# Where the context's tiles begin modulo 512 bytes in a two-block transformer kernel

## The reference

```python
# block 1 (depth 1)
h = rmsnorm(x) * (1 + sc1) + sh1
proj = h @ w_in                      # attention, gated delta rule
x = x + g1 * (concat(y_attn, y_delta) @ w_out)
x = x + g2 * ((silu(h2 @ w_gate) * (h2 @ w_up)) @ w_down)
x = rmsnorm(x)
# block 2, for i in range(2); m from c, mc from c_ctx
h  = ffn_half_step(h,  ..., w13_ffn1[i], w2_ffn1[i])   # sequence, 512 tokens
hc = ffn_half_step(hc, ..., w13_ffn1[i], w2_ffn1[i])   # context, 256 tokens
z  = modulate(rms_norm(h),  ...) @ w_in[i]
zc = modulate(rms_norm(hc), ...) @ w_in[i]             # last layer: key and value columns only
k, v from z and zc; y = concat(fourier(z), attend(q, k, v), sgu(z), pooling(z)) @ w_out[i]
h  = h + m[5] * y
h  = ffn_half_step(h, ..., w13_ffn2[i], w2_ffn2[i])
# the same mixer and second half step for the context, in layer 0 only
```

## The kernel before, in words

| tile | before | after the edit |
|---|---|---|
| weight slots `high`, `low`, `stage`, `tmp`, `eye`, `ones` | 128 | 128 |
| sequence: `hn`, `hidden`, `mixed` | 384 | 384 |
| context: `hn`, `hidden`, `mixed` (from `phase_base`, and in the mixer) | 64 | 384 |
| `keys`, `values`, `token_dft`, first `weights_t` of the context | 64 | 384 |
| `queries`, `scores` and `weights_t` of the sequence, `q_rank`, `fourier`, `rope` | 448 | 256 |
| first block: `attention_out`, `silu_z`, `delta_qkv` | 64 | 384 |

## Time and profile before

### The profile page before, as it was taken

One profiled execution on the slowest core, in us unless ns is written; L12 is line 12 of the kernel. 1 busy time (PEld: TensorE's weight loads), 2 busy tenths in 40 slices (PEclk: granted clock), 3 DMA queues, 4 the chain that ended last, 5 costly groups with the idle time before them and its releaser, 6 DMA issues. The chain is left out here.

```text
span 3632.5 us, 49233 instructions
## 1 busy us (share of the span) xinstructions
PE 3440.5 (95%) x19911; PEld 2834.4 (78%) x19911; DVE 2148.4 (59%) x4936; ACT 1031.5 (28%) x1604; POOL 131.9 (4%) x116
## 2 busy tenths in 40 slices
PE   5889889999999999899999999989999999999998
PEld 4655867887888888774688888878888886578887
DVE  6454656567667575764455767676766636544334
ACT  3354023222421212242432121222122125432222
POOL 0012010000000000100000000010000010000000
PEclk9998879999999999898999999989999999999999
DMA  8532024444234343330023434333333313023331
GB/s 176 146 95 67 3 58 131 121 132 112 86 99 116 99 114 95 99 87 17 24 64 99 111 93 115 97 107 87 106 105 103 106 53 110 13 73 95 94 104 64
DMA packets 646938, 333.94 MB, mean 92 GB/s; under 512 B 31659, under 2 KB 642935, under 8 KB 646456
## 3 DMA queue, kind: packets, MB, share of 16 engines
q1 hardware_dynamic: 645812, 330.63, 33.3%
q10 hardware_dynamic: 900, 0.18, 0.0%
HBM read 328.61 MB, written 2.77 MB: 91 GB/s over the span
## 5 line engine op out<-in xcount | busy, mean ns | idle before, releaser
L2105 PE MATMUL psum<-hn_high,high 128*128 128x512 f32 (+1 forms) x3136 | 1117.7, 356 | 9.4 <-DVE low L2550 9.3
L2107 PE MATMUL psum<-hn_high,low 128*128 128x512 f32 (+1 forms) x3136 | 1107.2, 353 | 0.0
L2106 PE MATMUL psum<-hn_low,high 128*128 128x512 f32 (+1 forms) x3136 | 1107.0, 353 | 0.0
L2635 DVE SCALAR_TENSOR_TENSOR partial<-stage,cond,partial 128x128 f32<-128x128 f32 x2592 | 701.8, 346 | 0.0
L2105 PEld LDWEIGHTS psum<-hn_high,high 128*128 128x128 f32 x3136 | 592.0, 189 | 116.1 <-issue 20.8
L2107 PEld LDWEIGHTS psum<-hn_high,low 128*128 128x128 f32 x3136 | 595.6, 190 | 82.0
L2106 PEld LDWEIGHTS psum<-hn_low,high 128*128 128x128 f32 x3136 | 591.7, 189 | 79.6 <-issue 0.5
L2550 DVE TENSOR_TENSOR low<-stage,high 128x1024 fp32r<-128x1024 f32 (+2 forms) x415 | 493.0, 1208 | 191.2 <-ACT high L1777 190.8
L1777 ACT ACTIVATE high<-stage 128x1024 fp32r<-128x1024 f32 (+2 forms) x415 | 415.3, 1025 | 500.5 <-DMA stage<-in_w_ffn 355.9
L2105 PE MATMUL psum<-hidden_high,high 128*128 128x512 f32 (+1 forms) x1408 | 496.4, 353 | 2.0 <-DVE hidden_low L2555 2.0
L2106 PE MATMUL psum<-hidden_low,high 128*128 128x512 f32 (+1 forms) x1408 | 494.6, 351 | 0.0
(11 more groups left out here) (316 smaller groups left out, 2962.6 us busy)
## 6 DMA issues: line engine op xcount, KB each, us to landing
stage<-in_w_ffn SPq DMA_DIRECT2D x240, 512.0 KB, 4.3
stage<-in_w_ada SPq DMA_DIRECT2D x768, 128.0 KB, 2.8
stage<-in_w_in SPq DMA_DIRECT2D x48, 512.0 KB, 4.6
stage<-in_w_out SPq DMA_DIRECT2D x24, 512.0 KB, 4.0
stage<-in_w_ffn SPq DMA_DIRECT2D x32, 384.0 KB, 3.8
stage<-in_w_gate SPq DMA_DIRECT2D x22, 512.0 KB, 4.0
stage<-in_w_up SPq DMA_DIRECT2D x22, 512.0 KB, 5.2
stage<-in_w_down SPq DMA_DIRECT2D x16, 512.0 KB, 3.9
```

Source lines behind the costliest of these rows:

```text
L2105: self.e.matmul(out, high[:, i], xh, start=first and n == 0, stop=False)
L2106: self.e.matmul(out, high[:, i], xl, start=False, stop=False)
L2107: done = self.e.matmul(out, low[:, i], xh, start=False, stop=last and n == nk - 1)
L2635: self.e.scalar_tensor_tensor(acc, view[:, k, :], by, acc, ALU.mult, ALU.add).then_inc(*inc)
```

## The change

The context's lane goes from 64 to 384. No other line is touched.

```diff
-ROW, MAIN_LANE, CTX_LANE = 512, 384, 64
+ROW, MAIN_LANE, CTX_LANE = 512, 384, 384
```

## The result

The changed kernel takes 3641.34 us (median of 6 runs, 3638.13 to 3646.21), the one before 3628.93 us in the same comparison (6 runs, 3625.87 to 3632.63). The ratio is 1.0036, with an interval of 1.0025 to 1.0046: the change costs 12.4 us, about 0.36%. The forecast of 3608 us, a gain of 21.8 us, was wrong, and wrong in its direction. One of the prediction's rivals, the fixed addition at 384, had been priced at 3641 us.

A forecast was written before the change was run, and what follows sets the result against it. TensorE was taken to bound the parts treating both token sets; 21.8 us less on the context's split matmuls and nothing elsewhere turned the 3630.06 us median into 3608 us (chance 0.50), with a range of 3602 to 3642 us.

The forecast's parts named there:

- the fixed addition at 384: Rival for the context's 256-column matmuls: 13.3 ns added whatever the columns, 120.0 ns each, +10.8 us, 3641 us; chance 0.15.
- What bounds the kernel: Where both token sets are treated, mainly 960 to 2960 us, TensorE is the limit; each matmul's nanoseconds count in the span.
- term 1: Context's split matmuls: pace falls from 117.8 to 113.3 ns, a sixteenth over streaming, on 4900 of them; 21.8 us less.
- The two arguments for the share: For a sixteenth: 512 columns keep 226.7 ns with every second group's loads at 40 columns; 256 columns also reach 113.3 ns.
- The price of the bound: Context's split matmuls: gain at least zero; an unsettled one costs about what they already do, so worse was not expected.
- The third rival: 13.3 ns at 384 is fixed, not a sixteenth: context's matmuls take 120.0 ns, +10.8 us, 3641 us; chance 0.15.
- Term 2: The sequence's own matmuls between the context's: addresses stay, pace stays 226.7 ns; taken at nothing.
- The second rival: The sequence stays unsettled at 231 ns after context groups: 4700 matmuls, 20.7 us more, 3651 us without context gain; chance 0.15.
- Term 3: Other matmuls on moved tiles (weights and values, keys and queries, scores), 640 counted: 2.8 us either way, taken at nothing.
- The rival that phase alone decides: Context's pace depends on the phase in which a stretch begins, not its address: nothing changes, 3630 us; chance 0.20.
- The rule of the Trainium skill: TensorE waits for no other reader and weight loads have their own port, so no address matters: sum 0, 3630 us.

The follow-up runs named there:

- experiment 5: Kernel before, the sequence's 512-column feed-forward matmuls of the first block cut into 384+128, 256+256 and 320+192 columns; no time given; 384 columns take 173.3 ns, 320 take 146.7.
- experiment 3: Kernel before, with the context's feed-forward tiles at other places modulo 512, in two scans; no time given; no place settled at 113.3 ns.
- experiment 4: Kernel before, with the sequence's feed-forward tiles at other places modulo 512 and the context still at 64; 3660.32 us against 3631.04, one run each.
- experiment 1: The change in two parts, against the kernel before at 3628.80 us: context's split tiles alone 3639.33 us (ratio 1.0031), base of the phases alone 3629.65 us (1.0002).
- experiment 2: Kernel before, with weights, context and sequence tiles all moved up by 64 bytes; 3629.74 us against 3628.80, ratio 1.0004.
- experiment 6: Changed kernel plus a second chain of the context's feed-forward products with 64, 96 or 32 weight columns; 4148.78 us, a time that means nothing here.

## Why the prediction was wrong

- **What bounds the kernel** was right. TensorE sets the end where the context's matmuls are, nothing covers it, and 2.1 ns on each of some 4900 gaps, 10.4 us, came out in the span. The loss lies between 960 and 2960 us and the lists of instructions are the same.
- **The step that failed** is in term 1: "It belongs to the streaming, then, and scales with the columns." The 13.3 ns of the earlier trace rows are fixed at that distance. 256 columns take 106.7 + 13.3 = 120.0 ns (experiment 5, and the timeline of after), not 113.3. The two arguments for the share both read something else. The earlier trace rows and the context of the earlier trace rows have 113.3 ns, but with the tiles at 64: distance 192 for the earlier trace rows, and 192 and 64 in turn for the earlier trace rows, whose blocks of 96 columns begin at 128 and 0 modulo 256. Neither stands behind a settled group of the sequence, and experiment 3 never gets that pace behind one. With the context at 384 the pace is gone in both cases: none of the full-width groups of after has it, and the 96-column context group of the earlier trace rows takes 117.9 ns there. The earlier trace rows change every second group of loads, with 512 columns; they could not say what a load does to 256. The two rows were joined into one rule although no row had the pair that was asked for, 256 columns at distance 0. The single-distance row, fits a fixed addition as well as a share.
- **The price of the bound** was wrong as well: "worse than now would need something that this trace does not show at 256 columns" took the absence of a row for a bound. The 13.3 ns of the earlier trace rows taken as fixed was such a row. The third rival used it and gave +10.8 us; the context's gaps measured +10.4, since each group's first two gaps stay short. That rival had nothing for the sequence, which adds 2.4 us, so its 3641 us meets the measured time in part by luck.
- **Term 2** was taken at nothing and is +2.4 us by the undisturbed gaps: after nearly every context group of the changed kernel five gaps are together some 27 ns longer than at 226.7. The second rival named the mechanism but had it last for the whole group, at 20.7 us. With the sequence at 384 it settles after five gaps; with the sequence at 0, 64 or 320 it would have lasted (experiment 4).
- **Term 3** was right: the base alone changes nothing that can be measured (experiment 1).
- **The rival that phase alone decides** was half right. What ran before does pick between 113.3 and 117.8 ns at 64, but the distance sets what can be had: under loads of 128 columns, no group at distance 0 in the trace of after settles below 119.3 ns, whatever ran before it.
- **The rule of the Trainium skill** that was weighed, by which no address could matter, would have given 3630 us. It is contradicted by the same kernel at 3641 and, with the distance restored, at 3631 us.

## What to carry to other kernels

A pace seen at one pair of operands is not to be carried to another: before a time is built on it, look for a row with the same number of moving columns, the same distance between moving tile and weights, and the same work ahead of it; where none exists, price a fixed addition and a proportional one with equal chance. Moving tiles and stationary tiles are placed together, since in this kernel their distance modulo 256 bytes sets the pace. And a distance that is good for 512 columns can be bad for 256.

## What the runs showed of the hardware

- Split matmuls of one form (128 weight columns, 256 moving columns, full clock) take 113.3, 116.7, 117.8, 118.2, 118.6, 119.8 or 120.0 ns from start to start once settled, by the distance of the moving tile from the weights modulo 256 bytes and by what ran before (experiments 3 and 4). 512 columns take 226.7, 229.2, or 233 to 234. Moving weights and moving tiles all by 64 changes nothing that was measured (experiment 2).
- At distance 0 the addition is 13.3 ns for 256, 320, 384 and 512 columns. With 128 or 192 moving columns the gap is 111.7 ns (experiment 5).
- The length of the weight load next to a 256-column matmul at distance 0 moves its gap: 120.0, 115.8, 113.3 and 117.8 ns for 128, 96, 64 and 32 columns (experiment 6). The Trainium skill, "TensorE: Matmul & The Clock Gate", Part 2, gives the load a port of its own that takes nothing from a running matmul; these gaps disagree.
- A stretch can keep a memory of the one before: with the same tiles at 64 the context settles at 117.8 ns behind every settled sequence of before and of experiment 4, and behind an unsettled one at 113.3 or at 117.8, by where that sequence stands and not by that alone (experiment 4). A sequence at 384 settles at once or after two to nine gaps, by the distance of the context ahead of it (experiment 3).

What stays open is the mechanism. The runs show that distance, load length and history set the gap together; they do not show which part of the memory or of TensorE the two reads share, why the period is 256 bytes, or why 32 weight columns are worse than 64.
